# Gate and up with x as the stationary operand, and a hidden product turned by 32x32 transposes on VectorE

## The chip, the cores and the metric

The kernel runs on one core of one Trainium2 chip. The metric is the time of one execution in microseconds (us), lower is better. Engines: TensorE (PE in the profile, its weight loads PEld), VectorE (DVE), ScalarE (ACT), GpSimd (POOL), and the DMA queue that SyncE (SP) feeds.

## The reference

256 tokens of width 1024 pass through three layers, all in float32. Each layer is: half a SwiGLU feed-forward, a mixer, and half a second feed-forward; the first two layers have a cross-attention to a memory of 256 rows before the second feed-forward. There are six feed-forwards ("ffn") of inner width 2816:

```python
def swiglu(x, w_gate, w_up, w_down):
    return (jax.nn.silu(x @ w_gate) * (x @ w_up)) @ w_down
x = x + 0.5 * swiglu(rmsnorm(x, g), w_gate, w_up, w_down)
```

The mixers (short convolution beside windowed attention; block attention; depthwise convolution beside gated linear attention) and a last gated projection are not touched, except that some semaphore counts change.

## The kernel before

**Precision.** Every operand of a large matmul is split in a high part (fp32r, written by ScalarE as a copy) and a low part (the rest, written by VectorE as a subtraction). A product is three matmuls into one PSUM bank: high x high, high x low, low x high. `products` (L1758 is its matmul) does so.

**Weights.** The weights are a sequence of units of 1 MB, in an order written out by hand (`units`, by `ffn_units` for an ffn). SP loads unit u into one of three slots (`raw`), once both halves of unit u - 3 are split. A unit has two halves of 128x1024; half v is split into one of SPL = 6 buffers of `w_hi` and `w_lo`. ScalarE's `split` (L612) waits for the load and for `half_done` of half v - 6; VectorE's (L1104) waits for the high part; TensorE's `split_ready` waits for the low part and its last matmul of the half adds to `half_done`. ScalarE and VectorE run the splits in a written order among their other work, LEAD = 5 halves ahead of the half that TensorE begins with.

**An ffn.** It runs over NJ = 11 steps j of 256 inner columns: gate (2 halves), up (2 halves), then the down projection of step j - 1 (2 halves). Gate and up have weights stationary and x moving: x turned lies as `xT[:, k, 0]` high beside `xT[:, k, 1]` low, so for each k and each 128 weight columns

```python
last = pe.matmul(bank[:, b, :], hi, xT[:, k, :, :], start=k == 0, stop=k == KD - 1)   # L1809, 512 columns
pe.matmul(bank[:, b, T:2 * T], lo, xT_hi[:, k, :], start=False, stop=False)           # L1808 or L1811, 256
```

gives the sum in two parts side by side in one bank (banks 0 to 3 for gate and up). Inner columns are on partitions, tokens on the free axis. ScalarE copies the second part out (L664, L668), VectorE adds the first (L1218, L1222). The norm's scale per token (`rstd`) varies along the free axis, so it is spread to a row: `diagonal` (L1164) makes diag(rstd), `scale_broadcast` (L1927) multiplies it by ones on TensorE, `scale_copy` (L1185) copies the row, and VectorE multiplies gate and up by it (L1226, L1230). Then ScalarE's silu (L672), VectorE's product (L1260), ScalarE's high part (`hid_hi`, L695) and VectorE's low part (`hid_lo`, L1265). Down (`row_half`) has the hidden tile stationary and 512 weight columns moving, into banks 4 to 7: 12 matmuls a half. `wide_rows`, used for values in the attention layers, has the same form with x stationary.

**Openings.** The first four halves of an ffn (`opening`) do k 0 to 3 first; x's last transposes (`rest_of_x`, L1886) come after two of these parts. `norm` on VectorE makes the low part of x, the split of half 4 and `rstd` (`rstd_of_both`, L1115 to L1126), then the ffn goes on with the split of half 5. The fifth ffn is late: two norms follow each other, so `first_norm` (L1173) rewrites x after the split of half 5 and the first sum, and `second_norm` makes the product of both scales; between them ScalarE squares the new x (`second_squares`, L624). The first ffn has an opening of its own, in quarters, with x and the weights loaded in parts (L410 to L418).

## Time and profile before

| | us |
|---|---|
| median of 3 timed runs | 1545.18 (1545.06 to 1545.27) |
| profiled execution, first to last instruction (its span) | 1543.2 |
| TensorE busy | 1533.1 (99%) |
| VectorE busy | 1111.1 (72%) |
| ScalarE busy | 833.6 (54%) |
| GpSimd busy | 83.8 (5%) |

The profile gives no time of the profiled execution beside its span; the timed runs are 2.0 us above the span. Busy is the share of the span in which an engine had an instruction running. Matmuls overlap, so the distance between two starts is shorter than one's duration, and a chain of work gives the distances.

### The profile page before, as it was taken

To read this page: it belongs to the slowest core of one execution; us is meant where nothing else is said; L and a number is where in the kernel's file an instruction comes from. 1 tells how busy PE (TensorE), PEld (TensorE's weight loads), DVE (VectorE), ACT (ScalarE), POOL (GpSimd) and SP (SyncE) were. 2 spreads that over 40 slices of the span, in tenths; PEclk is the share of its full clock that TensorE was granted. 3 is DMA by queue.
4 is the path that set the end of the run, shared out by engine and by line. 5 is a ranking of instruction groups with operands and counts; after the bars stand their busy time and mean duration, and the time that the engine had idled before them with its cause. 6 is when DMAs were issued, how large, how long until landed. Compare 5 with 4: busy or idle time off the path is not lost.

```text
span 1543.2 us, 23159 instructions
## 1 busy us (share of the span) xinstructions
PE 1533.1 (99%) x8920; PEld 1335.5 (87%) x8920; DVE 1111.1 (72%) x1568; ACT 833.6 (54%) x1168; POOL 83.8 (5%) x195
## 2 busy tenths in 40 slices
PE   9999999999999999999999999999999999999998
PEld 7888899988888888889988888888888997888886
DVE  6687779667666776666756876678766789876676
ACT  6565456555445555455555654455555564554555
POOL 0500002000000000000000081000000000000000
PEclk9999999999999999999999999999999999999999
DMA  8865653546555565554535556546655473655551
GB/s 303 237 227 193 192 164 137 191 137 205 203 190 171 165 218 182 196 189 163 175 123 164 188 166 214 190 141 205 217 190 176 149 219 100 212 196 197 190 191 55
DMA packets 207585, 282.46 MB, mean 183 GB/s; under 512 B 5578, under 2 KB 179528, under 8 KB 207512
## 3 DMA queue, kind: packets, MB, share of 16 engines
q1 hardware_dynamic: 202880, 274.51, 53.3%
q0 software_dynamic: 1584, 3.83, 0.9%
q10 hardware_dynamic: 3048, 3.11, 0.8%
q8 instruction: 50, 0.82, 0.2%
q14 instruction: 23, 0.19, 0.0%
HBM read 279.92 MB, written 3.08 MB: 183 GB/s over the span
## 4 chain that ended last, share of the span: by engine, by line
PE 97%; DVE 1%; ACT 1%; DMA 0%; issue 0%; SPq 0%; DVEq 0%; ACTq 0%
PE bank L1758 44%; PE bank L1809 32%; PE bank L1808 14%; PE bank L1811 2%; PE bank L1886 1%; PE bank L2048 1%; PE bank L2019 1%; PE bank L2277 1%; PE bank L2037 1%; DVE w_lo L1104 0%; DMA x<-in_x 0%; PE bank L1927 0%; PE bank L2027 0%; DVE arena L1701 0%; DVE x L1702 0%; ACT arena L1037 0%
## 5 line engine op out<-in xcount | busy, mean ns | idle before, releaser
L1104 DVE TENSOR_TENSOR w_lo<-raw,w_hi 128x1024 fp32r<-128x1024 f32 x514 | 615.4, 1227 | 213.3 <-ACT w_hi L612 212.8
L1809 PE MATMUL bank<-xT,w_hi 128*128 128x512 f32 x2112 | 733.6, 397 | 0.0
L612 ACT ACTIVATE w_hi<-raw 128x1024 fp32r<-128x1024 f32 x514 | 526.7, 1051 | 153.4 <-PE bank L1809 79.0
L1808 PE MATMUL bank<-xT,w_lo 128*128 128x256 f32 x1848 | 516.7, 280 | 0.0
L1809 PEld LDWEIGHTS bank<-xT,w_hi 128*128 128x128 f32 x2112 | 383.3, 188 | 73.5 <-DVE w_lo L1104 0.3
L1808 PEld LDWEIGHTS bank<-xT,w_lo 128*128 128x128 f32 x1848 | 348.6, 189 | 12.1 <-DVE w_lo L1386 0.3
L1758 PE MATMUL bank<-w_hi,hid_hi 128*128 128x512 f32 x524 | 205.7, 393 | 0.0
L1758 PE MATMUL bank<-w_hi,hid_lo 128*128 128x512 f32 x524 | 204.4, 390 | 0.0
L1758 PE MATMUL bank<-w_lo,hid_hi 128*128 128x512 f32 x524 | 204.2, 390 | 0.0
L1758 PE MATMUL bank<-xT,w_hi 128*128 128x256 f32 x816 | 148.7, 285 | 0.0
L1758 PEld LDWEIGHTS bank<-xT,w_hi 128*128 128x128 f32 x816 | 127.7, 192 | 0.9 <-issue 0.3
L695 ACT ACTIVATE hid_hi<-arena 128x512 fp32r<-128x512 f32 x66 | 41.8, 633 | 141.6 <-DVE arena L1260 141.6
L672 ACT ACTIVATE arena<-arena 128x512 f32<-128x512 f32 x66 | 41.7, 632 | 141.4 <-DVE arena L1226 141.4
L1758 PEld LDWEIGHTS bank<-w_hi,hid_lo 128*128 128x128 f32 x524 | 98.4, 188 | 20.8
L1758 PEld LDWEIGHTS bank<-w_lo,hid_hi 128*128 128x128 f32 x524 | 98.5, 188 | 20.3
L1758 PE MATMUL bank<-xT,w_lo 128*128 128x256 f32 x408 | 115.6, 283 | 0.0
L1758 PEld LDWEIGHTS bank<-w_hi,hid_hi 128*128 128x128 f32 x524 | 98.4, 188 | 17.9 <-issue 0.2
L664 ACT ACTIVATE arena<-bank 128x512 f32<-128x512 f32 x66 | 39.2, 594 | 77.1 <-PE bank L1809 77.1
L1758 PEld LDWEIGHTS bank<-xT,w_lo 128*128 128x128 f32 x408 | 78.2, 192 | 0.0
L1218 DVE TENSOR_TENSOR arena<-bank,arena 128x512 f32<-128x512 f32 x66 | 45.6, 690 | 45.1 <-ACT arena L664 45.1
L1811 PE MATMUL bank<-xT,w_lo 128*128 128x256 f32 x264 | 73.4, 278 | 0.0
L1265 DVE TENSOR_TENSOR hid_lo<-arena,hid_hi 128x512 fp32r<-128x512 f32 x66 | 45.8, 693 | 37.8 <-ACT hid_hi L695 37.7
(301 smaller groups left out, 1519.3 us busy)
## 6 DMA issues: line engine op xcount, KB each, us to landing
raw<-in_ffn_w_down SPq DMA_DIRECT2D x44, 1024.0 KB, 5.5
raw<-in_ffn_w_in SPq DMA_DIRECT2D x44, 1024.0 KB, 5.1
raw<-in_ffn_w_gate SPq DMA_DIRECT2D x43, 1024.0 KB, 5.4
raw<-in_ffn_w_up SPq DMA_DIRECT2D x43, 1024.0 KB, 5.4
raw<-in_ffn_w_out SPq DMA_DIRECT2D x22, 1024.0 KB, 5.3
raw<-in_w_in SPq DMA_DIRECT2D x10, 1024.0 KB, 5.2
raw<-in_xa_w_kv SPq DMA_DIRECT2D x8, 1024.0 KB, 5.2
raw<-in_od_w_in SPq DMA_DIRECT2D x8, 1024.0 KB, 5.5
```

The source lines that it names most:

```text
L612: act.activation(hi, src, ACT.Copy).then_inc(sem["hi_ready"], 1)
L664: act.activation(gate_part[:, :, :], bank[:, 0:2, T:2 * T], ACT.Copy).then_inc(sem["gate_part_ready"], 1)
L672: act.activation(act_gate[:, jb, :], act_gate[:, jb, :], ACT.Silu).then_inc(sem["act_gate_ready"], 1)
L695: act.activation(hid_hi[:, 2 * jb:2 * jb + 2, :], hidden[:, jb, :].rearrange("p (s t) -> p s t", s=2), ACT.Copy).then_inc(sem["hidden_hi_r ...
L1104: dve.tensor_tensor(lo, src, hi.bitcast(F32), ALU.subtract).then_inc(sem["lo_ready"], 1)
L1218: dve.tensor_tensor(gate, bank[:, 0:2, 0:T], gate_part[:, :, :], ALU.add).then_inc(sem["gate_summed"], 1)
L1265: dve.tensor_tensor(hid_lo[:, 2 * jb:2 * jb + 2, :], hidden[:, jb, :].rearrange("p (s t) -> p s t", s=2), hid_hi[:, 2 * jb:2 * jb + 2, :]. ...
L1758: last = pe.matmul(dst, lhs[l], rhs[r], start=start and n == 0, stop=stop and n == 2, skip_group_check=shared)
L1808: pe.matmul(bank[:, b, T:2 * T], lo, xT_hi[:, k, :], start=False, stop=False)
L1809: last = pe.matmul(bank[:, b, :], hi, xT[:, k, :, :], start=k == 0, stop=k == KD - 1)
L1811: pe.matmul(bank[:, b, T:2 * T], lo, xT_hi[:, k, :], start=False, stop=False)
L1886: last = pe.transpose(bank[:, k, t * P:(t + 1) * P], x[:, t, k * P:(k + 1) * P], ident[:, :])
```

## The change

Gate and up now have x stationary (one token tile of 128, high or low) and 512 weight columns moving, by `products` into one bank per token tile: tokens are on partitions. An ffn is five blocks of 512 inner columns and one of 256, whose gate and up columns share a bank. ScalarE's silu reads gate from PSUM with `rstd` as a scale per partition; VectorE multiplies by up from PSUM and by `rstd`. The product has tokens on partitions, so 16 VectorE transposes a block, each of 32 partitions into a quadrant of `hid_T` (8 tiles of 32x32 each, 4 in the last block), turn it for down. A block has one high and one low part of the hidden. The row of scales, its diagonals and its broadcast go in all six ffns. The opening does its first eight halves in the order gate, up (k 0 to 3), gate, up (k 4 to 7), both token tiles in each. The loads at the start, and the places of the squares and of the second norm in the late ffn, change with it. `first_half(b)` is `8 + 12 * (b - 1) if b else 0`.

```diff
 UC = 256
-NJ = FF // UC
+BLOCK = 512
+NB = 6
+LAST_FF = 5 * BLOCK
 HALF = 1024
 
...
-        for j in range(1, NJ):
-            col_unit(gate, j * UC)
-            col_unit(up, j * UC)
-            row_unit(down, (j - 1) * UC)
-        row_unit(down, (NJ - 1) * UC)
+        for k in (0, 4):
+            block_unit(gate, k, 0)
+            block_unit(up, k, 0)
+        for b in range(1, NB - 1):
+            for w in (gate, up):
+                for k in (0, 4):
+                    block_unit(w, k, b * BLOCK)
+            for r in (0, UC):
+                row_unit(down, (b - 1) * BLOCK + r)
+        for k in (0, 4):
+            units.append((BOTH, [w.rearrange("(k p) f -> p k f", p=P)[:, k:k + 4, LAST_FF:FF] for w in (gate, up)]))
+        for r in range((NB - 2) * BLOCK, FF, UC):
+            row_unit(down, r)
 
     ffns = []
 
...
-                    x_rows = a["x"][0].rearrange("(t p) d -> p t d", p=P)
-                    for n in range(4):
-                        part = slice(n * UC, (n + 1) * UC)
-                        sp.dma_start(x[:, :, part], x_rows[:, :, part]).then_inc(sem[f"x{n}_loaded"], 16)
-                        landing = raw_ready[slot] if n == 3 else sem[f"first{n}_loaded"]
-                        sp.dma_start(dst[:, 2 * n:2 * n + 2, :], src[:, 2 * n:2 * n + 2, :]).then_inc(landing, 16)
+                    for k in range(2):
+                        load_x(k)
+                        if k == 0:
+                            sp.dma_start(dst[:, 0:1, :], src[:, 0:1, :]).then_inc(sem["first0_loaded"], 16)
+                            sp.dma_start(dst[:, 1:2, :], src[:, 1:2, :]).then_inc(sem["first1_loaded"], 16)
+                        else:
+                            sp.dma_start(dst[:, 2:4, :], src[:, 2:4, :]).then_inc(raw_ready[slot], 16)
                     return
                 if u == 1:
-                    sp.dma_start(dst[:, 0:4, :], src[:, 0:4, :]).then_inc(sem["second_part_loaded"], 16)
-                    sp.dma_start(dst[:, 4:KD, :], src[:, 4:KD, :]).then_inc(raw_ready[slot], 16)
+                    sp.dma_start(dst[:, 0:2, :], src[:, 0:2, :]).then_inc(sem["second_part_loaded"], 16)
+                    sp.dma_start(dst[:, 2:4, :], src[:, 2:4, :]).then_inc(raw_ready[slot], 16)
+                    for n in range(2, 4):
+                        load_x(n)
                     return
...
+            def ffn_block(f, b, i=None, first=None, after=None, opened=0):
+
+                base = f.v0 + first_half(b) + LEAD
                 plus = (lambda k, n: k if i is None else k + n * i)
...
+                n_splits = 8 if b == 0 else (9 if b == NB - 1 else 12)
+                gate_at = 4 if b else 6
 
                 def silu():
...
+                    act.wait_ge(sem["half_done"], plus(f.v0 + first_half(b) + gate_at, LOOP_HALVES))
+                    if f.b0 or b:
+                        act.wait_ge(sem["hidden_ready"], plus(2 * (f.b0 + b), 2))
+                    if f.late and b == 0:
+                        act.wait_ge(sem["late_rstd_ready"], 1)
+                    n = UC if b == NB - 1 else BLOCK
+                    for t in range(NT):
+                        act.activation(act_gate[:, t, 0:n], bank[:, t, 0:n], ACT.Silu, scale=rstd[:, t:t + 1])\
+                            .then_inc(sem["gate_done"], 1)
+
+                def hidden_high(tiles, src_tiles):
+                    act.wait_ge(sem["hid_T_ready"], plus(f.b0 + b + (1 if b == NB - 1 and tiles.start else 0), 1))
+                    act.activation(hid_hi[:, tiles, :], hid_T[:, src_tiles, :], ACT.Copy).then_inc(sem["hidden_hi_ready"], 1)
+
+                if first is not None:
+                    first()
+                for n in range(n_splits):
+                    if n == gate_at:
+                        silu()
                     split(i, base + n)
...
             def second_norm():
                 rstd_of_both()
-                link(dve.tensor_tensor(rstd, rstd, first_rstd, ALU.mult))
-                diagonal()
+                link(dve.tensor_tensor(rstd, rstd, first_rstd, ALU.mult), "late_rstd_ready")
 
...
+            def hidden_product(f, b, i):
+
+                n = UC if b == NB - 1 else BLOCK
+                done = 8 if b and b < NB - 1 else (4 if b else 8)
+                dve.wait_ge(sem["half_done"], f.v0 + first_half(b) + done if i is None
+                            else f.v0 + first_half(b) + done + LOOP_HALVES * i)
+                for t in range(NT):
+                    ready = 2 * (f.b0 + b) + t + 1
+                    dve.wait_ge(sem["gate_done"], ready if i is None else ready + 2 * i)
+                    up = bank[:, t, UC:2 * UC] if b == NB - 1 else bank[:, 2 + t, :]
+                    dve.scalar_tensor_tensor(hidden[:, t, 0:n], up, rstd[:, t:t + 1], act_gate[:, t, 0:n],
+                                             ALU.mult, ALU.mult).then_inc(sem["hidden_ready"], 1)
+                ready = 2 * (f.b0 + b) + 2
+                dve.wait_ge(sem["hidden_ready"], ready if i is None else ready + 2 * i)
+
+            def hidden_transposes(b, rows):
+
+                g = 32
+                n_tiles = 2 if b == NB - 1 else 4
+                by_block = hidden.rearrange("p t (s c i) -> p c t s i", s=4, c=4)
+                by_token = hid_T.rearrange("p s (t q i) -> p q t s i", t=NT, q=4)
+                for q in rows:
+                    for c_ in range(4):
+                        last = dve.transpose(by_token[c_ * g:(c_ + 1) * g, q, :, 0:n_tiles, :],
+                                             by_block[q * g:(q + 1) * g, c_, :, 0:n_tiles, :])
+                if rows[-1] == 3:
+                    last.then_inc(sem["hid_T_ready"], 1)
+
+            def hidden_low(f, b, i):
+
+                ready = f.b0 + b + 1
+                dve.wait_ge(sem["hidden_hi_ready"], ready if i is None else ready + i)
+                tiles, src = (slice(4, 6), slice(0, 2)) if b == NB - 1 else (slice(0, 4), slice(0, 4))
+                dve.tensor_tensor(hid_lo[:, tiles, :], hid_T[:, src, :], hid_hi[:, tiles, :].bitcast(F32), ALU.subtract)\
+                    .then_inc(sem["hidden_lo_ready"], 1)
+
+            def ffn_block(f, b, i=None, late=False, first=None, after=None, before_residual=None):
+
+                base = f.v0 + first_half(b) + LEAD
+                n_splits = 8 if b == 0 else (9 if b == NB - 1 else 12)
+                if first is not None:
+                    first()
+                if late:
+                    first_norm()
+                split(i, base)
+                if late:
+                    second_norm()
+                if b:
+                    hidden_low(f, b - 1, i)
+                n = 1
+                if b == NB - 1:
+                    for n in range(1, 4):
+                        split(i, base + n)
+                    hidden_product(f, b, i)
+                    hidden_transposes(b, (0, 1, 2, 3))
+                    split(i, base + 4)
+                    hidden_low(f, b, i)
+                    for n in range(5, 8):
+                        split(i, base + n)
+                    if before_residual is not None:
+                        before_residual()
+                    add_residual(0.5, between=lambda: split(i, base + 8))
                 else:
...
+                    for n in range(1, 8):
                         split(i, base + n)
...
+                    hidden_product(f, b, i)
+                    if b:
+                        split(i, base + 8)
+                    hidden_transposes(b, (0, 1))
+                    if b:
+                        split(i, base + 9)
+                    hidden_transposes(b, (2, 3))
+                    for n in range(10, n_splits):
                         split(i, base + n)
+                if after is not None:
...
+                def block_tile(v, b, t, k, kk):
+                    return products(bank[:, b + t, :], tuple(m[:, k, t * P:(t + 1) * P] for m in X), w_cols(v, kk, 512),
+                                    k == 0, k == KD - 1)
+
+                def block_half(v, b, n, i=None):
+                    split_ready(v, i)
+                    for t in range(NT):
+                        for kk in range(2):
+                            last = block_tile(v, b, t, 2 * n + kk, kk)
+                    last.then_inc(sem["half_done"], 1)
+
+                def gate_up(b, i=None, before_up=None):
+                    v = v0 + first_half(b)
+                    ready = 2 * (b0 + b)
+                    pe.wait_ge(sem["gate_done"], ready if i is None else ready + 2 * i)
+                    if b == NB - 1:
+                        pe.wait_ge(sem["hidden_ready"], ready)
                     for n in range(4):
...
+                        block_half(v + n, 0, n, i)
+                    if b == NB - 1:
                         return
...
+                    pe.wait_ge(sem["hidden_ready"], ready if i is None else ready + 2 * i)
+                    if before_up is not None:
+                        before_up()
+                    for n in range(4):
+                        block_half(v + 4 + n, 2, n, i)
+
+                def down(b, i=None, v=None, between=None):
+                    ready = b0 + b + 1
+                    pe.wait_ge(sem["hidden_lo_ready"], ready if i is None else ready + i)
+                    if b == NB - 1:
+                        last_rows(v, HID, 4)
                         return
...
+                    for s in range(4):
+                        row_half(v + s, d_bank, HID, s, b == 0 and i is None and s == 0, False, i)
+                        if s == 1 and between is not None:
                             between()
...
+                def first_halves(n_half):
+                    v = v0 + n_half
+                    n, b = 2 * (n_half // 4) + n_half % 2, 2 * (n_half // 2 % 2)
+                    if first_transposes is not None and n_half == 0:
+                        pe.wait_ge(sem["first_lo_ready"], 1)
+                    else:
+                        split_ready(v, None)
+                    for t in range(NT):
+                        for kk in range(2):
+                            if b == 0 and t == 0:
+                                c.next("xT_lo_ready")
+                            if first_transposes is not None and (n_half, t, kk) == (0, 0, 1):
+                                split_ready(v, None)
+                            last = block_tile(v, b, t, 2 * n + kk, kk)
+                    last.then_inc(sem["half_done"], 1)
+
+                for n in range(8):
+                    if n == 2:
+                        if first_transposes is not None:
+                            first_transposes(2)
+                            first_transposes(3)
                         else:
...
+                            rest_of_x()
+                    first_halves(n)
                 if late:
                     c.skip("residual", 4)
                 if first_up is not None:
                     first_up()
+
```

The calls of `diagonal()` ahead of the other five ffns are removed too; `silu` on ScalarE stands before the split of half `gate_at` of a block, and `first` of the late ffn is `second_squares`.

## Rows read from the trace of the kernel before

**Rows 1.** Page: span, busy time of engines, granted clock in 40 slices.
```profile
span 1543.2 us, 23159 instructions
...
PE 1533.1 (99%) x8920; PEld 1335.5 (87%) x8920; DVE 1111.1 (72%) x1568; ACT 833.6 (54%) x1168; POOL 83.8 (5%) x195
...
PEclk9999999999999999999999999999999999999999
```

**Rows 2.** Page: the chain that ended last, by engine and by line.
```profile
PE 97%; DVE 1%; ACT 1%; DMA 0%; issue 0%; SPq 0%; DVEq 0%; ACTq 0%
PE bank L1758 44%; PE bank L1809 32%; PE bank L1808 14%; PE bank L1811 2%; PE bank L1886 1%; PE bank L2048 1%; PE bank L2019 1%; PE bank L2277 1%; PE bank L2037 1%; DVE w_lo L1104 0%; DMA x<-in_x 0%; PE bank L1927 0%; PE bank L2027 0%; DVE arena L1701 0%; DVE x L1702 0%; ACT arena L1037 0%
```

**Rows 3.** Groups by line and shape, TensorE: busy us, mean ns | idle before.
```profile
L1809 PE MATMUL bank<-xT,w_hi 128*128 128x512 f32 x2112 | 733.6, 397 | 0.0
L1808 PE MATMUL bank<-xT,w_lo 128*128 128x256 f32 x1848 | 516.7, 280 | 0.0
```

**Rows 4.** Chain in order of time: start us, us, line, instructions.
```profile
339.29 0.87 PE bank L1886 x8
...
360.20 5.46 PE bank L1758 x24
376.85 5.44 PE bank L1758 x24
...
509.86 8.17 PE bank L1758 x36
...
710.64 14.39 PE bank L1758 x120
...
1029.10 1.39 PE bank L1758 x6
```

**Rows 5.** Timeline, TensorE, wide_rows: start us, us; 12 and 33 matmuls lie between.
```profile
748.04 0.39 PE L1758 MATMUL bank<-w_lo,xT 128*128 128x512 f32 x1
...
750.81 0.39 PE L1758 MATMUL bank<-w_lo,xT 128*128 128x512 f32 x1
...
758.29 0.39 PE L1758 MATMUL bank<-w_lo,xT 128*128 128x512 f32 x1
```

**Rows 6.** Groups by line and shape, VectorE (columns as in rows 3).
```profile
L1104 DVE TENSOR_TENSOR w_lo<-raw,w_hi 128x1024 fp32r<-128x1024 f32 x512 | 614.0, 1229 | 212.0 <-ACT w_hi L612 211.6
...
L1218 DVE TENSOR_TENSOR arena<-bank,arena 128x512 f32<-128x512 f32 x66 | 45.6, 690 | 45.1 <-ACT arena L664 45.1
...
L1350 DVE TENSOR_SCALAR arena<-arena,small 128x256 f32<-128x256 f32 x32 | 10.9, 384 | 0.6
```

**Rows 7.** Timelines of VectorE (four splits; fifth ffn), ScalarE (fifth ffn).
```profile
1311.86 4.62 DVE L1104 TENSOR_TENSOR w_lo<-raw,w_hi 128x1024 fp32r<-128x1024 f32 x4
...
1037.56 0.16 DVE L1115 TENSOR_SCALAR small<-small 128x2 f32<-128x2 f32 x1
...
1039.74 1.23 DVE L1104 TENSOR_TENSOR w_lo<-raw,w_hi 128x1024 fp32r<-128x1024 f32 x1
...
1041.48 2.73 DVE L1173 SCALAR_TENSOR_TENSOR x<-x,small,gain_row 128x512 f32<-128x512 f32 x4
1044.13 0.16 DVE L1175 COPY small<-small 128x2 f32<-128x2 f32 x1
...
1043.14 1.05 ACT L624 ACTIVATE arena<-x 128x1024 f32<-128x1024 f32 x1
...
1045.43 1.05 ACT L612 ACTIVATE w_hi<-raw 128x1024 fp32r<-128x1024 f32 x1
```

**Rows 8.** Start: timeline of TensorE; GB/s in 40 slices of 0:30.
```profile
6.29 1.07 PE L1886 MATMUL bank<-ident,x 128*128 128x128 f32 x4 [0.27 <-DMA x<-in_x]
...
7.23 0.48 PE L1809 MATMUL bank<-xT,w_hi 128*128 128x512 f32 x1
...
GB/s 0 0 8 148 325 350 287 259 311 363 340 359 359 375 363 354 350 350 348 350 345 350 348 363 392 410 415 399 410 421 373 304 321 224 280 306 326 280 273 360
```

**Rows 9.** Page: DMA issues, KB each, us to landing.
```profile
raw<-in_ffn_w_gate SPq DMA_DIRECT2D x43, 1024.0 KB, 5.4
```

454 lines of the change are left out of this document (132 added, 322 removed).

## Prediction, on record before the result

> **What bounds the kernel now.** I read the page's engine table first. TensorE is busy for 1533.1 of 1543.2 us at full granted clock, VectorE for 72% and ScalarE for 54% [rows 1]. Then the chain of work that ended last: 97% of it is TensorE, in two line groups, L1758 (weight or token tiles by `products`; 44%) and L1808 to L1811 (gate and up; 48%) [rows 2]. So the time is the number of matmuls times the distance between two starts, and another engine matters only where it makes TensorE wait. The durations in the groups (397 and 280 ns) are no distances, because matmuls overlap: 2112 and 1848 of these alone sum to 1250 us [rows 3]. Distances come from the chain in order of time. In the second ffn the down halves begin every 16.626 us (376.85 to 509.86 is eight steps), and 24 matmuls of 512 columns take 5.44 us, 226.7 ns each; 120 of 256 columns take 14.39 us, 119.9 ns each [rows 4]. Two of 256 cost 13.1 ns more than one of 512, so an instruction has a fixed part of some 13 ns beside its columns.
>
> One gate and up step is thus 16.626 - 5.44 = 11.186 us for 32 pairs of a 512 and a 256 matmul: 349.6 ns a pair.
>
> **The change, part by part.**
>
> *Matmuls.* For one k and 512 weight columns, before needs 4 pairs (3072 columns in 8 instructions) and after 2 token tiles x 3 products of 512 (3072 columns in 6). The columns are the same; a quarter of the instructions goes, 4224 to 3168 in all. The new form is already in this kernel: wide_rows has x stationary and 512 weight columns moving, with the same three products in the same order, and from 750.81 to 758.29 33 such matmuls start 226.7 ns apart [rows 5]. The twelve before them (748.04 to 750.81), behind 256-column work, are 231 apart. So a 512 block costs 96 x 0.2267 = 21.76 us, against 2 x 11.186 = 22.37. That is 0.61 us saved, times 5.5 blocks times 6 ffns: **-20.0 us**. At the pair's own rate per column, 349.6 x 512/768 = 233 ns, it would be 22.37 a block and nothing saved; that is the bound from above. I take 226.7, since all of an ffn is then 512 wide, as down is.
>
> A rule speaks against this term. The Trainium skill (TensorE: Matmul & The Clock Gate, Back-to-back issue gap) gives N/2.4 + 2.5 ns for a warm matmul. By that, before is 1300 ns for a k and 512 columns and after 1295, and the 528 of them would save 2.8 us instead of 20. The trace differs: 13 ns, not 2.5 [rows 4]; what the rule would give is weighed as rival D.
>
> *Scale broadcasts.* Six diagonals and their broadcast matmuls go. From the end of x's last transposes in the second ffn (339.29 + 0.87) to the first down half (360.20) there are 20.04 us; 56 pairs are 19.58, so the broadcast takes 0.46 [rows 4]. Six: **-2.8 us**. The six DVE diagonals and copies lie beside PE.
>
> *VectorE.* Per 512 block there go ten passes of 512 elements (two sums from PSUM, two scales and a product, twice), 0.69 us each (L1218 is one of them, [rows 6]), and two hid_lo of 0.69. There come two products from PSUM (0.69), one hid_lo of 1024 (1.23) and 16 transposes of 32 partitions x 256 elements. No row has a transpose. Passes of 1024 and 512 elements give a slope of (1229 - 690)/512 = 1.05 ns an element and a fixed part of 0.15 us, so 0.42 for 256; L1350 takes 0.38 [rows 6]. From below it is one start, 0.16 us, as the 2-element steps have [rows 7]; from above, if the 32x32 blocks were filled and drained without overlap, each element is paid twice, 0.69 us. I take 0.42, 6.8 us a block. Sum per block: 12 splits x 1.15 (four take 4.62 us, [rows 7]) + 1.4 + 1.2 + 6.8 = 23.2 us, against 32.6 of PE (21.76 + 10.88 of down). It is hidden. Four splits in a row overlap by 0.07 us each (1.155 apart, 1.229 long); the transposes are counted without that.
>
> The Trainium skill (VectorE: DVE Perf Modes, Two Vector instructions with no wait between them) says an instruction whose start quadrant differs from the last one's waits until all earlier ones have finished. Each transpose writes to another quadrant than the one before, so by it they would not overlap, which is how they are counted; with overlap the 16 would be 1.1 us shorter and slack longer. No row of before shows it.
>
> Where would the transposes show? PE's halves take 2.72 us, and six split buffers mean that a split can be five halves ahead. In the steady blocks splits stand between the transposes: product, split, 8 transposes, split, 8 transposes, three splits; the farthest delay is about 8 us of the 13.6 of lead. In block 0 there are none between. From the opening's start, half 8 begins at 8 x 2.72 + 0.87 (x's transposes) = 22.6 us; DVE then makes the product (1.4), 16 transposes T and the split of half 13 (1.2), which PE wants at 36.2. Slack is 11.0 - 16T: 4.3 us at T = 0.42, gone at 0.69. In the last block the hidden product starts as down(4) begins, with 10.9 us for the product (0.9), 16 transposes of 128 elements (0.15 + 128 x 1.05 ns = 0.28 each), a split (1.2) and hid_lo (0.7), 7.3 in all: covered. The loads keep their size and number (three slots of 1 MB), and land in 5.4 us [rows 9].
>
> *ScalarE* loses four copies a block and has the silu and the high part as before; at 54% [rows 1] it is no bound.
>
> *Where the change adds waits.* The scale per token is now needed before the silu, and in each block 0 rstd stands ahead of the split of half 5. In a common ffn that costs nothing: in the fifth one's rows rstd ends at 1039.74 and the split could end at 1040.9 [rows 7], wanted at 1045.0. But this ffn is the late one, with two norms. Its opening starts at 1029.10 + 1.39 = 1030.5 [rows 4]; half 5 starts 5 x 2.72 + 0.87 later, at 1045.0. In DVE's order first_norm starts at 1039.74 (where the split of half 5 stood) and lasts 2.65 [rows 7]. ScalarE's two squares of the new x now stand ahead of its high part of half 5: they start after the first two passes (1041.15), the second waits for the fourth pass (1042.4) and ends at 1043.5 (a square is 1.05 [rows 7]); high part 1.05, low part 1.2: ready at 1045.8, **0.9 us late**. second_norm's 12 steps (2.4 us) then stand ahead of half 6: lo at 1049.3, and PE wants it at 1045.8 + 2.72: **0.8 us late**. Queued behind are halves 7 on, which are ready in time. Together +1.7.
>
> *The start.* The queue's order changes: the second quarter of x is now the fourth load of 256 KB, not the third, and TensorE waits for it before its first product. It is there at 6.29 and the first product starts at 7.23 before; the loads bring some 350 GB/s [rows 8], so 0.6 to 0.75 us later: +0.6. Half 1 then needs 512 KB in one piece and a whole split of 1024 (1.05 + 1.23 instead of 0.63 + 0.69): landed about 8.7, low part done 11.0, while half 0 ends at 7.8 + 2.72 = 10.5: +0.5. Halves 2 on are covered: x's second half has landed when half 1 ends at 14, the transposes take 1.2 more, ScalarE's high parts of x and of half 4 end at 17.0, the squares take 2.3 (1043.14 to 1045.43) and rstd 2.2 (1037.56 to 1039.74) [rows 7], so half 5's split ends at 22.8, wanted at 15.0 + 3 x 2.72 = 23.2. Together +1.2 (0 to 4, the bound being a unit's landing more).
>
> **Sum**, against the profiled span of 1543.2 us: 1543.2 - 20.0 - 2.8 + 1.7 + 1.2 = 1523.3 us. The median of the timed runs, 1545.18, lies 2.0 above the span, so **1525.3 us**, 1.3% faster.
>
> **Rivals.**
>
> A: no stall at all, late and start included. That is 1522.4; it lies within the forecast's own range of 1521 to 1530.
>
> B: VectorE comes late, so that part of the gain goes. Place: block 0 of each ffn, half 13's split behind 16 transposes. For it: nothing between them there, and no row for a transpose. Against: T has to be over 0.69, above every row of 256. At T = 0.80 the stall is 1.8 us six times: 1525.3 + 10.8 = 1536.
>
> C: slower than before. The same place with T past 0.90: 16T - 11.0 = 3.4 us a time, 20 in all, takes the gain. At T = 1.0 it is 30 us and the steady block is 16.4 + 16 = 32.4 of VectorE against 32.6 of PE, so nothing is caught up: 1525.3 + 30 = 1555. Against it: 0.90 is twice 0.42, and above the 0.69 of paying each element twice. The Trainium skill (Vector Engine (DVE) Microarchitecture Reference, 3.8) says the transposing front end sustains an element per cycle per lane, which would be the 0.42.
>
> D: the width buys nothing; the fixed part is not what the pairs lose, and the new matmuls start 233 ns apart. No gain there: 1545.2 - 2.8 + 2.9 = 1545.3, no change. For it: the twelve of [rows 5] at 231. Against: down's halves and the other 33 stand at 226.7. The Trainium skill's formula for the gap (the TensorE page named above), with a saving of 2.8 for the width, would end near it, at 1542.5.
>
> **How the numbers follow.** Forecast with A: 77%. B 10%, C 6%, D 4%, the rest 3% for a wait I do not see, most of it still faster. Range: the bounds of the start (0 to 4) and of the late ffn (0 to 3) give 1522 to 1530, half of B takes it to 1534; 1521 to 1534 leaves out about 17%. Two in a thousand, 3 us, is about what a measurement tells here from no change. Faster is forecast, A, B and part of the rest: 0.89. Same: D, 0.04. Slower: C and a little, 0.07.
>
> **What the profile after would show.** 3168 matmuls of 512 in one gate and up line, starts 227 ns apart; blocks 32.6 us apart in each ffn; no L1927 in the ffns; transposes at about 0.42 us, and no idle PE behind the low splits except in the late ffn's opening (two waits under 1 us) and in the first 12 us. Wrong it would be by transposes over 0.7 us, by starts at 233, or by idle PE at block 1.

## The result, and the profile after

The changed kernel takes **1531.46 us** (median of four runs, 1530.2 to 1532.57) against 1545.22 before on the same chip: ratio 0.9909, 95% interval 0.9895 to 0.9923. The forecast was 1525.3, its range 1521 to 1534: the kernel gained 13.8 us where 19.9 were forecast. The four runs lie in two pairs 2.2 us apart (1530.2 and 1530.4, 1532.52 and 1532.57); the profiled execution is of the lower pair, 1530.2 us with a span of 1528.5. The forecast of the span was 1523.3, so 5.2 us are to be found.

The page of the changed kernel (span, engines, chain by engine and by line), to be held against [rows 1, 2]:

```profile
span 1528.5 us, 21035 instructions
...
PE 1511.7 (99%) x7852; PEld 1283.7 (84%) x7852; DVE 1166.5 (76%) x1837; ACT 768.0 (50%) x1011; POOL 76.0 (5%) x195
...
PE 95%; DVE 2%; ACT 1%; DMA 1%; issue 0%; SPq 0%; DVEq 0%; ACTq 0%
PE bank L1741 90%; PE bank L1835 1%; PE bank L2009 1%; PE bank L1980 1%; DMA raw<-in_ffn_w_gate 1%; DVE w_lo L1104 1%; PE bank L2238 1%; PE bank L1998 1%; ACT w_hi L632 0%; PE bank L1988 0%; DVE arena L1684 0%; ACT xT L660 0%; DVE x L1173 0%; DVE x L1685 0%; ACT arena L1037 0%
```

All of an ffn is one line of TensorE now, but the chain has gone from 97% TensorE to 95%, with VectorE, ScalarE and a transfer in the rest. The chain in order of time (start, us, line, instructions) says where:

```profile
33.05 65.58 PE bank L1741 x288
...
341.33 171.41 PE bank L1741 x756
...
522.74 171.41 PE bank L1741 x756
...
842.54 171.41 PE bank L1741 x756
...
1029.53 2.75 DVE x L1173 x4
...
1035.78 165.12 PE bank L1741 x720
```

In the three common ffns 756 matmuls stand in one unbroken piece, 171.41 / 756 = 226.7 ns apart, the distance taken from [rows 4, 5]. The late ffn's 720 need 165.12 us, 229.3 ns each, 1.9 us more than 720 x 226.7 = 163.2.

A mark lets the ffns be compared one by one: TensorE's first transposes of x, just before an ffn ends. First two of before, around the late ffn, then the same two of after (timelines: start us, us):

```profile
1026.66 0.60 PE L1886 MATMUL bank<-ident,x 128*128 128x128 f32 x4
...
1211.89 0.60 PE L1886 MATMUL bank<-ident,x 128*128 128x128 f32 x4
```

```profile
1013.79 0.60 PE L1835 MATMUL bank<-ident,x 128*128 128x128 f32 x4
...
1200.75 0.60 PE L1835 MATMUL bank<-ident,x 128*128 128x128 f32 x4
```

| from mark to mark | before | after | change |
|---|---|---|---|
| start to the first ffn's end | 192.15 | 190.66 | -1.49 |
| fourth ffn (841.47 and 832.38 to the rows above) | 185.19 | 181.41 | -3.78 |
| late (fifth) ffn | 185.23 | 186.96 | +1.73 |

A common ffn saves 3.8 us; the forecast had (20.0 + 2.8) / 6 = 3.8. The late ffn is 186.96 - 181.41 = 5.5 us above an undisturbed one where 1.7 was forecast, and the first ends 2.3 us after 192.15 - 3.79 where 1.2 was forecast. These two, 3.8 and 1.1, are 4.9 of the 5.2 us. Inside them stand four idle times of TensorE that are over a microsecond or near it, of which the first is the opening wait for x that before has too (timeline of after; in brackets the wait and what ended it):

```profile
6.79 0.66 PE L1835 MATMUL bank<-ident,x 128*128 128x128 f32 x4 [0.74 <-DMA x<-in_x]
...
11.40 0.50 PE L1741 MATMUL bank<-w_hi,xT 128*128 128x512 f32 x1 [1.08 <-DVE w_lo L1104]
...
33.05 0.50 PE L1741 MATMUL bank<-w_hi,xT 128*128 128x512 f32 x1 [1.35 <-ACT arena L689]
...
1035.78 0.50 PE L1741 MATMUL bank<-w_hi,xT 128*128 128x512 f32 x1 [3.63 <-DVE w_lo L1104]
```

The matmul in front of the last of these starts at 1031.76, so 4.02 us lie between two starts, 3.8 more than 0.23. And the granted clock fell behind it (stretches of after: PE, PEld, DVE, ACT, POOL busy, then the clock):

```profile
1031.00:1036.00 5.00, 1.37 (x7) 0.82 (x6) 2.81 (x6) 4.83 (x7) 0.00 (x0) 1.00 0.32 105
1036.00:1041.00 5.00, 5.00 (x16) 3.96 (x16) 4.62 (x14) 2.19 (x3) 0.00 (x0) 0.66 0.69 210
1041.00:1050.00 9.00, 9.00 (x41) 7.43 (x40) 7.06 (x9) 5.18 (x6) 0.00 (x0) 1.00 0.94 337
```

A mean of 0.66 is a stretch of which about two thirds ran at 1.2 GHz. That, with a small wait near 1040 us, is the 1.9 us that the 720 matmuls lost.

Why were they late? The late ffn, VectorE then ScalarE:

```profile
1026.21 1.23 DVE L1104 TENSOR_TENSOR w_lo<-raw,w_hi 128x1024 fp32r<-128x1024 f32 x1 [0.38 <-ACT w_hi L632]
...
1029.53 2.74 DVE L1173 SCALAR_TENSOR_TENSOR x<-x,small,gain_row 128x512 f32<-128x512 f32 x4
...
1034.50 1.23 DVE L1104 TENSOR_TENSOR w_lo<-raw,w_hi 128x1024 fp32r<-128x1024 f32 x1 [2.15 <-ACT w_hi L632]
...
1030.98 1.06 ACT L644 ACTIVATE arena<-x 128x1024 f32<-128x1024 f32 x1 [4.80 <-DVE x L1173]
...
1033.36 2.93 ACT L632 ACTIVATE w_hi<-raw 128x1024 fp32r<-128x1024 f32 x3
```

This is the chain of the forecast, first_norm, squares, high part and low part of half 5, in its order. But first_norm starts 1029.53 - 1017.6 = 11.9 us after the opening, not the 9.2 that the forecast took over from the kernel before. The second half of x's transposes stands after two halves, and a half now lasts 2.72 us where the opening of before had half-units of 1.4, so x's second part, the split of half 4 and rstd all moved 2.7 us back.

The start, ScalarE of after:

```profile
26.74 2.01 ACT L632 ACTIVATE w_hi<-raw 128x1024 fp32r<-128x1024 f32 x2 [4.44 <-DMA raw<-in_ffn_w_gate]
29.36 1.06 ACT L632 ACTIVATE w_hi<-raw 128x1024 fp32r<-128x1024 f32 x1 [0.61 <-DMA raw<-in_ffn_w_gate]
30.44 1.28 ACT L689 ACT_TABLE_LOAD   x1
31.73 1.26 ACT L689 ACTIVATE arena<-bank,small 128x512 f32<-128x512 f32 x2
```

The first silu stands behind splits whose weights have not landed, and is preceded by a table load of 1.28 us; TensorE needs the gate's banks for block 1 and waits for it.

VectorE's price, in groups (busy, mean ns) and in the start's timeline:

```profile
L1228 DVE STREAM_TRANSPOSE arena<-arena 32x256 f32<-32x256 f32 x480 | 209.2, 436 | 6.8
```

```profile
37.70 7.18 DVE L1228 STREAM_TRANSPOSE arena<-arena 32x256 f32<-32x256 f32 x16
```

Sixteen take 7.18 us, 0.449 apart; 0.42 was taken.

### The profile page after: what moved, and what is told of

Same layout as the page of the kernel before. It is cut to its first block, busy times and chain, and to the rows that moved or that the text cites. A ratio compares the mean times of both kernels' runs of the same rounds, so it can differ in the third digit from the quotient of the medians.

```text
span 1528.5 us, 21035 instructions
## 1 busy us (share of the span) xinstructions
PE 1511.7 (99%) x7852; PEld 1283.7 (84%) x7852; DVE 1166.5 (76%) x1837; ACT 768.0 (50%) x1011; POOL 76.0 (5%) x195
## 4 chain that ended last, share of the span: by engine, by line
PE 95%; DVE 2%; ACT 1%; DMA 1%; issue 0%; SPq 0%; DVEq 0%; ACTq 0%
PE bank L1741 90%; PE bank L1835 1%; PE bank L2009 1%; PE bank L1980 1%; DMA raw<-in_ffn_w_gate 1%; DVE w_lo L1104 1%; PE bank L2238 1%; PE bank L1998 1%; ACT w_hi L632 0%; PE bank L1988 0%; DVE arena L1684 0%; ACT xT L660 0%; DVE x L1173 0%; DVE x L1685 0%; ACT arena L1037 0%
## 5 line engine op out<-in xcount | busy, mean ns | idle before, releaser
L1741 PE MATMUL bank<-w_hi,xT 128*128 128x512 f32 (+1 forms) x2304 | 711.8, 387 | 6.1 <-DVE w_lo L1104 4.7
L1741 PEld LDWEIGHTS bank<-w_hi,xT 128*128 128x128 f32 x2304 | 431.4, 188 | 95.2 <-DVE w_lo L1104 5.6
L1741 PE MATMUL bank<-w_lo,xT 128*128 128x512 f32 (+1 forms) x1152 | 445.7, 387 | 0.0
L1741 PEld LDWEIGHTS bank<-w_lo,xT 128*128 128x128 f32 x1152 | 216.7, 188 | 43.6
L1228 DVE STREAM_TRANSPOSE arena<-arena 32x256 f32<-32x256 f32 (+1 forms) x576 | 238.3, 414 | 8.2
L1741 PEld LDWEIGHTS bank<-xT,w_hi 128*128 128x128 f32 x816 | 127.6, 191 | 1.0 <-issue 0.3
L1741 PE MATMUL bank<-xT,w_lo 128*128 128x256 f32 x408 | 115.4, 283 | 0.0
L1741 PEld LDWEIGHTS bank<-xT,w_lo 128*128 128x128 f32 x408 | 78.1, 191 | 0.0
L689 ACT ACTIVATE arena<-bank,small 128x512 f32<-128x512 f32 (+1 forms) x72 | 42.8, 646 | 37.3 <-PE bank L1741 37.2
L1215 DVE SCALAR_TENSOR_TENSOR arena<-bank,small,arena 128x512 f32<-128x512 f32 (+1 forms) x72 | 47.5, 701 | 13.3 <-PE bank L1741 7.8
```

The costliest lines, as they stand in the source:

```text
L689: act.activation(act_gate[:, t, 0:n], bank[:, t, 0:n], ACT.Silu, scale=rstd[:, t:t + 1])\
L1215: dve.scalar_tensor_tensor(hidden[:, t, 0:n], up, rstd[:, t:t + 1], act_gate[:, t, 0:n], ALU.mult, ALU.mult).then_inc(sem["hidden_ready"], 1)
L1228: last = dve.transpose(by_token[c_ * g:(c_ + 1) * g, q, :, 0:n_tiles, :], by_block[q * g:(q + 1) * g, c_, :, 0:n_tiles, :])
L1741: last = pe.matmul(dst, lhs[l], rhs[r], start=start and n == 0, stop=stop and n == 2, skip_group_check=shared)
```

## Experiments

Theory: the 5.2 us are waits of TensorE at two places, the late ffn's opening and the start. Rivals: transposes that hold VectorE up; matmuls that start farther apart than thought. Twelve kernels ran. The table has their numbers (median of four runs, for the half doubling of eleven; ratio to the kernel before on the same chip with its interval; span, first ffn's end and late ffn's length from the profile). The runs were on several chips, on which the kernel before had medians of 1545.22 to 1546.22 us; so where one kernel is held against another below, "on its own chip" means that each is first held against the kernel before beside it (the changed kernel is 13.76 us faster so counted):

| run | us | ratio | span | first ends | late ffn |
|---|---|---|---|---|---|
| changed kernel | 1531.46 | 0.9909 (0.9895 to 0.9923) | 1528.5 | 190.66 | 186.96 |
| e1_rest_early | 1529.20 | 0.9889 (0.9873 to 0.9906) | 1528.8 | 194.32 | 183.46 |
| e2_late_order | 1528.81 | 0.9883 (0.9867 to 0.9900) | 1530.0 | 195.41 | 183.56 |
| e3_load_order | 1530.18 | 0.9898 (0.9882 to 0.9915) | 1531.0 | 193.23 | 186.81 |
| e7_all | 1525.95 | 0.9876 (0.9859 to 0.9892) | 1524.3 | 189.99 | 183.39 |
| e4_narrow | 1572.80 | 1.0180 (1.0163 to 1.0197) | 1571.3 | | |
| e5_transposes_twice | 1605.22 | 1.0382 (1.0364 to 1.0399) | 1603.2 | 208.83 | 197.50 |
| e6_same_quadrant | 1531.93 | 0.9908 (0.9892 to 0.9925) | 1531.4 | 193.63 | 186.93 |
| e8_silu_early | 1529.46 | 0.9893 (0.9878 to 0.9908) | 1527.5 | 189.75 | 186.93 |
| e9_best | 1525.38 | 0.9866 (0.9851 to 0.9881) | 1523.6 | 188.95 | 183.80 |
| e10_half_twice | 1548.57 | 1.0017 (1.0008 to 1.0026) | 1546.3 | 199.07 | 188.40 |
| e11_best_rest_early | 1522.37 | 0.9852 (0.9836 to 0.9869) | 1520.2 | 188.01 | 181.40 |
| e12_two_moves | 1525.45 | 0.9869 (0.9853 to 0.9886) | 1523.8 | 189.38 | 183.56 |

Intervals of single mends (e1, e2, e3, e8) overlap with the changed kernel's, so their verdicts rest on their profiles, not on their medians.

**e1_rest_early**: x's second half after one half of products in the late ffn.

```diff
-                    if n == 2:
+                    if n == (1 if late else 2):
                         ...
                             rest_of_x()
```

> The changed kernel, with x's last transposes of the late ffn put after one half of its opening instead of two. Theory (the prediction's sum for the late ffn left out that the transposes now come after two whole halves, 5.4 us, where before they came after 2.8; all of VectorE's chain behind them is 2.7 us later): half 5's wait falls from 3.8 to about 1.1 us, half 6's stays under 1, and the time falls by 2.7 us from 1531.5 to about 1528.8. Rival (the squares and the norm on ScalarE and VectorE alone set the wait, wherever the transposes stand): no change.

The late ffn falls from 186.96 to 183.46 us; its two waits are 0.92 us at 1036.71 and 0.50 at 1040.23, both on w_lo, and first_norm starts at 1030.45, 9.2 us after the opening at 1021.3. On its own chip this kernel gains 3.3 us over the changed one, where 2.7 were expected. The place of the transposes made the forecast's 1.7 us into 5.5: with it mended, 2.0 are left.

**e2_late_order**: the splits of halves 5 and 6 ahead of first_norm and second_norm on VectorE, ScalarE's squares behind two splits.

```diff
-                if late:
-                    first_norm()
                 split(i, base)
                 if late:
+                    first_norm()
+                    split(i, base + 1)
                     second_norm()
```

> The changed kernel, with the splits of halves 5 and 6 of the late ffn put ahead of the rewriting of x and the squares, as the order was before. Theory (both waits of the late opening come only from splits queued behind the norm): no wait of TensorE over 0.2 us between 1020 and 1045, time 4.2 us less, about 1527.3. Rival (the silu, which now needs the late scale, takes the place of the wait): a wait of some 1 to 3 us before the gate of block 1, time 1 to 3 us less.

The 3.63 us wait is gone, and the late ffn takes 183.56; later ones came (0.48 us at 1043.07, 0.77 at 1060.48), the first of them against the expectation; no wait on the silu took its place. On its own chip the gain is 3.7 us, of 4.2 expected. In this profile the silu's wait was longer than in the changed kernel's, and the clock fell there as well (timeline, and a stretch of e2_late_order):

```profile
35.01 0.80 PE L1743 MATMUL bank<-w_hi,xT 128*128 128x512 f32 x1 [2.85 <-ACT arena L689]
```

```profile
36.00:38.00 2.00, 2.00 (x6) 1.59 (x5) 2.00 (x2) 1.97 (x4) 0.00 (x0) 0.50 0.25 96
```

Nothing up to the first silu differs between the changed kernel, e1, e2 and e6 (e6 changes the transposes behind it); the first ffn's end lies at 190.66, 194.32, 195.41 and 193.63. So the start is worth 2.3 us in one execution and up to 7 in another. The transfers' landing decides: ScalarE's first waiting split starts at 26.74, in e2 at 28.67.

**e3_load_order**: in the first ffn five weight units, not four, ahead of memory, sinks, final gain and rank weights; block 1's loads are written out ahead of the loop.

```diff
-                    for n in range(first_units):
+                    for n in range(first_units + (1 if u == 0 else 0)):
```

> The changed kernel, with the loads of the memory, the sinks and the gain row issued after five weight units instead of four, as before the change. Theory (the fifth and sixth unit land behind 1.5 MB of other loads, the first silu stands behind a split that waits for them): ScalarE's waits for weights of 4.4 and 0.6 us before 30 us and TensorE's 1.5 us at 31.3 go, time 1.5 us less, about 1530.0. Rival (the DMA queues are full all the time until 30 us, so the order only moves the wait): the first silu is as late, no change.

The waits that were to go stayed, so that a median near the expected 1530.0 shows nothing for the theory: TensorE still waits 2.09 us for the silu at 34.01. Five splits do run in one piece now (19.61 to 24.45), but the silu stands behind the sixth, of a unit whose load is not issued before 23.17 us (some 23.1 in the changed kernel too), and that one waits (ScalarE of e3_load_order):

```profile
19.61 4.84 ACT L636 ACTIVATE w_hi<-raw 128x1024 fp32r<-128x1024 f32 x5
30.32 1.06 ACT L636 ACTIVATE w_hi<-raw 128x1024 fp32r<-128x1024 f32 x1 [5.88 <-DMA raw<-in_ffn_w_gate]
31.40 1.28 ACT L693 ACT_TABLE_LOAD   x1
```

So moving the small loads does not take the wait away; that the silu's place in ScalarE's order does is what e8 tests.

**e7_all**: e2 and e3, and the first unit's second half loaded and split in two pieces.

```diff
+                            sp.dma_start(dst[:, 2:3, :], src[:, 2:3, :]).then_inc(sem["first2_loaded"], 16)
+                            sp.dma_start(dst[:, 3:4, :], src[:, 3:4, :]).then_inc(raw_ready[slot], 16)
```

> Both orders put back (splits ahead of the late norm; five units ahead of the memory), and half 1 of the start loaded and split in two pieces of 512 columns. Theory (the three places are all that the changed kernel loses against the sum of matmuls): 4.2 + 1.5 + 1.2 us less, about 1524.5, 20.7 less than before the change. Rival (one wait is covered by another): 1526 to 1529.

1525.95 us, just below the rival's range and above the theory's 1524.5. The wait of 1.08 us at 11.40 is gone, one of 0.34 at 22.53 came, and the silu's 1.38 stayed; TensorE's clock is 1.00 from 32 to 45 us.

**e4_narrow**: each gate and up product cut in two of 256 columns, so that the instructions go from 3168 to 6336 with the same columns.

```diff
+                        for h in range(2):
+                            last = pe.matmul(bank[:, b + t, h * T:(h + 1) * T], X[l][:, k, t * P:(t + 1) * P],
+                                             w_cols(v, kk, 512)[r][:, h * T:(h + 1) * T],
```

> The changed kernel, with each gate and up matmul of 512 moving columns cut in two of 256 (same stationary tile, same columns in all, 6336 instructions instead of 3168). Theory (an instruction costs some 13 ns beside its columns): starts 120 ns apart, 3168 x 13.1 ns = 41.5 us more, about 1573. Rival (an instruction costs 2.5 ns beside its columns, as the Trainium skill, TensorE: Matmul & The Clock Gate, Back-to-back issue gap, has it): 8 us more, 1539. Second rival (the width has no part in the gain): no change.

1572.8 - 1531.46 = 41.3 us over 3168 more instructions is 13.0 ns each (40.8 us and 12.9 ns with each on its own chip), and a piece of the chain of e4_narrow has 192 in 23.03 us, 119.9 ns each:

```profile
67.76 23.03 PE bank L1889 x192
```

The fixed part of 13 ns of [rows 4] holds. The Trainium skill (TensorE: Matmul & The Clock Gate, Back-to-back issue gap) gives 2.5 ns, as the gap of a matmul taken by itself, which would have been 8 us; the trace does not agree here, where each matmul of 256 or 512 columns has a weight load of its own.

**e5_transposes_twice** and **e10_half_twice**: all sixteen transposes of a block, or eight of them, made a second time into scratch that nothing reads.

```diff
+                        if c_ < 2:          # e10 alone
+                            dve.transpose(by_spare[c_ * g:(c_ + 1) * g, q, :, 0:n_tiles, :],
+                                          by_block[q * g:(q + 1) * g, c_, :, 0:n_tiles, :])
```

> The changed kernel with every transpose done twice, the extra one into a spare part of the arena (32 instead of 16 a block). Theory (the slack of VectorE in block 0 is 11.0 us less the transposes, 7.2 now): 13 to 14.3 us of transposes, half 13's split 2 to 3.3 us late in each ffn and a third of a microsecond in the other blocks, in all 12 to 27 us more, 1544 to 1558. Rival (VectorE's work is hidden with much more room than that, as its 76% busy share would say): under 3 us more.

> Eight of the sixteen transposes of a block are made a second time, into a part of the scratch that nothing reads: VectorE has 24 x 0.449 = 10.8 us of them in a block in place of 7.2. Theory 1 (VectorE has room of 11.0 us against 16 transposes, as the forecast worked it out for block 0 and more for the others, so 24 at 0.449 fit by 0.2 us): nothing in the loop's blocks, and one wait of up to 1.5 us in an ffn where the room is smallest: 1531.5 to 1537. Theory 2 (the room is smaller than worked out, as the run with all sixteen doubled, 74 us slower, suggests, 18 of the 36 to 74 lying in waits that the sum did not have): half of that run's loss, 1555 to 1570.

They cost 74 and 17 us. The first is above its expectation, the second lies between its two theories. In the second ffn of e5 TensorE waits twice, behind block 0's transposes and in the last block on the low part of hidden, where the sum had 7.3 of 10.9 us for sixteen transposes (timeline of e5_transposes_twice):

```profile
393.95 0.80 PE L1745 MATMUL bank<-w_hi,xT 128*128 128x512 f32 x1 [4.46 <-DVE w_lo L1104]
...
538.56 0.79 PE L1745 MATMUL bank<-w_hi,hid_hi 128*128 128x512 f32 x1 [3.51 <-DVE hid_lo L1242]
```

```profile
393.00:396.00 3.00, 2.05 (x5) 1.67 (x6) 3.00 (x3) 3.00 (x4) 0.00 (x0) 0.50 0.29 30
396.00:400.00 4.00, 4.00 (x14) 3.16 (x13) 3.66 (x4) 3.56 (x5) 0.00 (x0) 0.69 0.88 316
400.00:410.00 10.00, 10.00 (x46) 8.26 (x45) 8.39 (x13) 4.33 (x6) 0.00 (x0) 1.00 0.87 304
```

Each brings a stretch at 1.2 GHz: from 393.95, where TensorE starts again, to 400 us it lost another 2.05 x 0.50 + 4 x 0.31 = 2.3 us. The six ffns have twelve such waits of 2.7 to 4.5 us, and with some 2 us of clock behind each they are most of the 74. In the steady blocks of the second ffn nothing waits, with 32 transposes in a block; in the first ffn, where VectorE also computes the norm of the memory, one wait of 2.38 us comes at 84.57. In e10 that one is 2.66 us, at 85.43, and the first ffn alone loses 8.4 of the 17 us. Its second ffn has one long wait, and the clock stays at 1.00 behind it:

```profile
370.23 0.43 DVE L1231 STREAM_TRANSPOSE arena<-arena 32x256 f32<-32x256 f32 x1
...
380.06 1.22 DVE L1104 TENSOR_TENSOR w_lo<-raw,w_hi 128x1024 fp32r<-128x1024 f32 x1
```

```profile
381.34 0.50 PE L1746 MATMUL bank<-w_hi,xT 128*128 128x512 f32 x1 [1.56 <-DVE w_lo L1104]
```

Here 24 transposes take 9.8 us and TensorE stands 1.97 - 0.23 = 1.7 us longer between two starts: the room is 8.1 us. Before the transposes VectorE's product starts 25.3 us after the opening (343.5 to 368.8), not 22.6, since two splits stand ahead of it whose high parts ScalarE makes only after the silu. The silu in turn stands behind a split whose load lands at 353.45, about a microsecond after TensorE is done with the gate, and behind a table load. In the changed kernel, ScalarE and then VectorE:

```profile
353.45 1.06 ACT L632 ACTIVATE w_hi<-raw 128x1024 fp32r<-128x1024 f32 x1 [5.16 <-DMA raw<-in_ffn_w_gate]
354.52 1.28 ACT L689 ACT_TABLE_LOAD   x1
355.82 1.27 ACT L689 ACTIVATE arena<-bank,small 128x512 f32<-128x512 f32 x2
356.98 2.95 ACT L632 ACTIVATE w_hi<-raw 128x1024 fp32r<-128x1024 f32 x3
...
358.07 2.36 DVE L1104 TENSOR_TENSOR w_lo<-raw,w_hi 128x1024 fp32r<-128x1024 f32 x2 [2.30 <-ACT w_hi L632]
360.35 1.40 DVE L1215 SCALAR_TENSOR_TENSOR arena<-bank,small,arena 128x512 f32<-128x512 f32 x2
361.79 7.19 DVE L1228 STREAM_TRANSPOSE arena<-arena 32x256 f32<-32x256 f32 x16
```

So of the room for sixteen transposes 0.9 us was left, not 4.3. The silus end at 357.09, some 0.4 us before TensorE writes block 1's gate to their banks: the wait that the first ffn has for the silu is near in this one too.

**e6_same_quadrant**: each transpose writes to the quadrant that it reads, so that hidden's tiles lie in another order and the output is not the reference's.

```diff
-                        last = dve.transpose(by_token[c_ * g:(c_ + 1) * g, q, :, 0:n_tiles, :],
+                        last = dve.transpose(by_token[q * g:(q + 1) * g, c_, :, 0:n_tiles, :],
```

> The changed kernel with each transpose written to the quadrant of partitions that it reads (so the hidden product is turned only within quadrants; the output isn't the reference's). Theory (Trainium skill, VectorE: DVE Perf Modes, Two Vector instructions with no wait between them: a change of quadrant makes the next instruction wait for the end of the last): 16 transposes take 5.9 to 6.1 us instead of 7.2, the time stays at 1531.5 within 1, since they are hidden. Rival (the distance between transposes has nothing to do with the quadrant): 7.2 us as now, same time.

The sixteen take 5.71 us instead of 7.18 (timeline of e6_same_quadrant), 0.357 apart, and the time is the same, 0.9908 against 0.9909:

```profile
39.07 5.71 DVE L1228 STREAM_TRANSPOSE arena<-arena 32x256 f32<-32x256 f32 x16
```

The crossing order costs 1.5 us a block, and it is hidden. What counts is the change from one transpose to the next, not that one reads and writes different quadrants: in e5 two that both read quadrant 0 and write quadrant 1 start at 381.00 and 381.37, 0.37 apart. The Trainium skill (VectorE: DVE Perf Modes, Two Vector instructions with no wait between them) has an instruction wait for the earlier ones when its start quadrant differs from the last one's; the trace agrees: with the change they start 0.449 us apart at a mean duration of 0.436, so they don't overlap, and in e6 0.357 apart at 0.404, so they do.

**e8_silu_early**: in the first ffn the silu is issued after three splits, and the program's first small activation is a silu, which loads the table.

```diff
+                silu_at = 3 if n_ffn[0] == 1 and b == 0 else gate_at
                 for n in range(n_splits):
-                    if n == gate_at:
+                    if n == silu_at:
                         silu()
...
-            act.activation(table_start[:, :], unit_sq[:, 0:1], ACT.Copy)
+            act.activation(table_start[:, :], unit_sq[:, 0:1], ACT.Silu)
```

> The changed kernel with the first silu alone moved: ScalarE issues it after three of its six splits in block 0 of the first ffn, ahead of those that wait for a transfer, with the same wait for TensorE's halves, and the small activation at the program's start is a silu, so that the 1.28 us table load at 30.44 us is made there instead of between the gate and block 1. Theory 1 (the silu stood behind splits that waited 4.44 and 0.61 us for their transfers, and TensorE behind it): the silu starts at 26 us, the 1.74 us gap of TensorE at 31.3 is gone (2.5 to 3.2 us in other runs, with granted clock at half level for 2 to 5 us behind it), and the time falls by 1.5 us in the mild executions and by up to 4 in the others: median 1528.5 (1527 to 1530), against 1531.5. Theory 2 (the weights themselves come late, and the split of block 1's first half is what TensorE would wait for next): a wait on w_lo of 1 to 2 us stands in place of the one on the silu, time within 0.7 us of 1531.5. The late ffn's wait of 4 us near 1032 to 1036 us stays in both, with the half level behind it for about 4 us.

The silu runs at 27.04, on TensorE's release, with no table load, and the five splits follow in one piece:

```profile
27.04 1.27 ACT L689 ACTIVATE arena<-bank,small 128x512 f32<-128x512 f32 x2 [3.99 <-PE bank L1742]
28.19 4.92 ACT L632 ACTIVATE w_hi<-raw 128x1024 fp32r<-128x1024 f32 x5
```

TensorE has no wait between 12 and 1030 us, and the first ffn ends at 189.75. The late ffn keeps its 3.63 us. The median, 1529.46, is a microsecond above the expected one and within its range; four runs span 1.25 us. The silu's move and the table's were not tried one by one.

**e9_best**: e7 and the silu's move.

```diff
+                silu_at = 5 if n_ffn[0] == 1 and b == 0 else gate_at
```

> All mends together: splits of halves 5 and 6 ahead of the two norms in the late ffn, a fifth weight unit ahead of the small loads, the first unit's second half loaded and split in two pieces, and the first silu ahead of the split of unit 5's first half, with its table loaded at the start. Its forerunner without the silu's move ran in 1525.95 with 1.38 us of wait on the silu. Theory 1 (the waits of TensorE are what the changed kernel lost against the 1522.4 us of the forecast's no-stall case): 1524.0 (1522.5 to 1525.5), no wait of TensorE over 0.7 us before 1300 us, clock 1.00 in every stretch. Theory 2 (something else, spread over the program, costs the rest): 1525.5 or more, with the waits gone all the same.

1525.38 us, at the upper end of Theory 1's range, but one of its conditions fails. The start is clean; two waits on w_lo stay in the late ffn, 0.46 us at 1036.61 and 1.03 at 1054.26, and it lasts 183.80: what is left of the loss lies there, which e11 tests.

**e11_best_rest_early**: e9 and e1 together.

> The best kernel so far with the second half of x's transposes in the late ffn put after one half's products again, 2.7 us earlier. By the starts of the x transposes the best kernel's late ffn takes 183.80 us against 181.41 for an undisturbed one, 2.4 us more, of which 0.62 and 1.19 us are waits on w_lo near 1036 and 1054 us. Theory 1 (these waits go back to the late norms, which then come 2.7 us earlier): the late ffn in 181.5 to 182.5 us, no wait of TensorE over 0.3 us between 1020 and 1060 us, time 1523.6 us (1523 to 1524.5). Theory 2 (VectorE is the bound there, with two norms and the splits in one stretch, whatever the start): one of the waits stays or moves later, late ffn over 183 us, time within 0.5 us of 1525.4.

The late ffn takes 181.40 us, an undisturbed one's 181.41, and between 22.25 and 1300 us TensorE has no wait. The clock stands at 1.00 where it had fallen (stretch of e11_best_rest_early):

```profile
1030.00:1045.00 15.00, 15.00 (x68) 12.41 (x67) 12.70 (x24) 7.12 (x9) 0.00 (x0) 1.00 0.67 248
```

At 1522.37 us (ratio 0.9852, 0.9836 to 0.9869) it beats both kernels, and lies 0.6 us below Theory 1's range; the span is 1520.2, against the 1520.4 (1543.2 - 22.8) that rival A gives.

**e12_two_moves**: e2 and e8 alone, two moves in two engines' orders.

> The changed kernel with two moves of order alone: the late ffn's splits ahead of its norms (1528.81 us by itself) and the first silu ahead of the splits that wait for transfers, with its table loaded at the start (1529.46 us by itself); 1531.46 us without either. Theory 1 (the two waits are separate losses): they add, 1526.8 us (1526 to 1527.8), with the runs within 1 us of each other. Theory 2 (one slow-down is shared, so that half of either gain is the other's): 1528 to 1529.

1525.45 us: 6.0 below the changed kernel, where the two alone gave 2.65 and 2.0 by their medians. That they seem to give more together comes from the chips: with each kernel on its own chip e2 gains 3.7 us, e8 2.8 and the two together 6.4. So the losses are separate and add, as Theory 1 has it, as far as e2's four runs, which span 5.8 us, can tell; its range of 1526 to 1527.8 was worked out from the medians and is missed for that reason.

## Why the prediction came out as it did

- **Matmuls, -20.0, and broadcasts, -2.8:** right. 226.7 ns in every unbroken piece and 3.78 us from a common ffn. Rival D is out by this, and e4 shows the fixed part of 13 ns. (The 2.8 us that the forecast worked out for the width by the rule with 2.5 ns is 528 x 5 ns = 2.6; this changes nothing.)
- **VectorE hidden:** right in outcome, with the size off. T was 0.449, not 0.42, and the product in block 0 starts 2.7 us later than worked out, because ScalarE puts a split that waits for its load, a 1.28 us table load and the silu ahead of the high parts that VectorE splits. The room was 8.1 us, so the threshold of rival B was T = 0.51, not 0.69: it was much nearer than 10% lets one think, and that T stayed below it is in part luck. Its price per stall was too low as well, since the clock falls behind long waits.
- **The late ffn, +1.7:** this step failed in size. It measured 5.5, above the bound of 3 that the forecast gave it. The order of the norms was right; what was missed is that rest_of_x counts halves and that a half had doubled (e1: 3.5 us come back), and that a wait of 3.6 us takes the clock with it (1.9 us).
- **The start, +1.2:** 2.3 in the profiled execution. The first product came at 7.31 us, not 0.6 late but 0.1; half 1 came 1.2 us late, not 0.5; and block 1 waited 1.35 us for the silu, a wait that the forecast did not have (e8 takes it away). It had called ScalarE no bound by its busy share of 54%, and that share does not tell what stands ahead of one instruction in the queue. These three sum to 2.8 between starts of matmuls, 0.5 more than the 2.3; that difference was not traced.
- **Span to median, +2.0:** 1.7 in the profiled run; the median stands 1.3 above that run. In profiles the first ffn's end varies by 4.8 us with the silu's wait. That the timed runs' two levels come from it is likely: e6, as fast as the changed kernel, was profiled in a run of 1533.17 us, and its span is 2.9 us longer, all of which lies before the first ffn's end (193.63 against 190.66); and the runs of e8 and of e12 lie within 1.3 us. It was not shown for the changed kernel itself, of which no run at 1532.5 was profiled, and e11, without that wait, still has one run 1.6 us above the others.
- **The range:** with the forecast's own bounds for the late ffn and the start it was 1522 to 1530, and 1531.46 lies above that. It is within 1521 to 1534 only because the top was moved up for rival B, which did not happen; that is luck, not the sum.

## What to carry to other kernels

When a unit of work changes size, look for every place that counts in that unit ("after two halves") and recompute when it now happens. A sum of hidden work must start from when its first instruction can start, behind everything in its own queue and in its releasers' queues, a table load too. Once the waits are found, moves of order, and here one load cut in two, cost TensorE nothing and gave a further 9 us, more than a third of what the whole change brings in e11.

## What the runs showed of the hardware

- Behind waits of TensorE of 1.35 us (after, 33.05) and 1.56 us (e10, 381.34) the granted clock stayed at 1.00; behind 3.63 us (after) it was 0.66 over the next 5 us, and behind 2.85 us (e2, 35.01) it was 0.50 until about 41 us, by the distances between starts. Each of the two waits thus cost about 6 us: 3.8 and 1.9 in the changed kernel, 3.0 and 3.0 in e2.
- Transposes of 32 partitions x 256 fp32 elements start 0.357 us apart when they read and write the quadrants of the last one (e6), and 0.449 apart when each writes to another quadrant than the last (after).
- A table load of 1.28 us for the silu serves the copies and squares that follow it as well: one made at the program's start (e8, 1.46) is the only one until 225.80 us, where the changed kernel has another at 30.44.
